# Split projections of a two-block network: the low part of each weight slice moves from VectorE to GpSimd

## The reference, cut to what matters

```python
k, v = jnp.split(mem_n @ w_kv, 2, axis=-1)                    # mkv, for both layers: 2 x (1024 x 512)
... = split_cols(h @ w_in, EVEN_SPLITS)                       # even_in: 1024 x 4096
return x + jnp.concatenate([y_a, y_b, y_m], axis=-1) @ w_out  # even_out: 1280 x 1024
return (gate * hs.astype(h.dtype)) @ w_out                    # lru_out: 1024 x 1024
return out @ w_o                                              # mla_out: 1024 x 1024

mod = (jax.nn.silu(c) @ ada_w[l] + ada_b[l])[:, None, :]      # modulation: 1024 x 6144, twice
shift, scale = jnp.split((jax.nn.silu(c) @ kv_ada_w + kv_ada_b)[:, None, :], 2, axis=-1)  # 1024 x 2048
```

## Time and profile before

| | us |
|---|---|
| median of 3 runs (range) | 2895.5 (2894.27 to 2897.55) |
| the profiled execution, its own time | 2892.08 |
| its span | 2890.4 |
| TensorE busy | 2405.4 (83%) |
| VectorE busy | 2093.0 (72%) |
| ScalarE busy | 1170.5 (40%) |
| GpSimd busy | 149.5 (5%) |

### The profile page before, as it was taken

One profiled execution on the slowest core, in us unless ns is written; L12 is line 12 of the kernel. 1 busy time (PEld: TensorE's weight loads), 2 busy tenths in 40 slices (PEclk: granted clock), 3 DMA queues, 4 the chain that ended last, 5 costly groups with the idle time before them and its releaser, 6 DMA issues. The chain is left out here.

```text
span 2890.4 us, 40401 instructions
## 1 busy us (share of the span) xinstructions
PE 2405.4 (83%) x11809; PEld 1961.6 (68%) x11809; DVE 2093.0 (72%) x4755; ACT 1170.5 (40%) x2040; POOL 149.5 (5%) x165
## 2 busy tenths in 40 slices
PE   4957892868374889999999995779479999999996
PEld 3745542737264778888888883467368888888885
DVE  4877788655669967777777774468977777777775
ACT  3526311410321854444444442351474444444443
POOL 0000000000002510000000000001430000000000
PEclk9978995789697999999999997899799999999998
DMA  6750661057230045555555553211015555555553
GB/s 236 254 207 1 222 216 72 30 189 259 76 124 1 0 153 189 189 190 190 191 192 190 193 182 106 88 59 45 0 53 194 192 192 190 189 189 189 190 191 113
DMA packets 159074, 428.05 MB, mean 148 GB/s; under 512 B 15348, under 2 KB 21776, under 8 KB 158992
## 3 DMA queue, kind: packets, MB, share of 16 engines
q1 hardware_dynamic: 158992, 427.09, 43.8%
HBM read 426.00 MB, written 1.05 MB: 148 GB/s over the span
## 5 line engine op out<-in xcount | busy, mean ns | idle before, releaser
L2133 PE MATMUL bank<-h_t_parts,u_t_high 128*128 128x512 f32 x2048 | 508.9, 391 | 10.2 <-DVE u_t_low L2219 10.2
L2133 PEld LDWEIGHTS bank<-h_t_parts,u_t_high 128*128 128x128 f32 x2048 | 386.2, 189 | 91.3 <-DVE u_t_low L2219 11.1
L2207 ACT ACTIVATE activated<-activated 128x256 f32<-128x256 f32 x256 | 107.1, 418 | 588.8 <-DVE activated L2232 588.8
L2219 DVE TENSOR_TENSOR u_t_low<-u_ring,u_t_high 128x1024 fp32r<-128x1024 f32 x256 | 312.9, 1222 | 28.2 <-ACT u_t_high L2197 16.8
L2146 PE MATMUL bank<-v_high,weighted_high 128*128 128x512 f32 x1024 | 319.4, 393 | 2.7 <-DVE weighted_low L2243 2.7
L2197 ACT ACTIVATE u_t_high<-u_ring 128x1024 fp32r<-128x1024 f32 x256 | 271.7, 1061 | 119.9 <-DMA u_ring<-in_peer_u 115.0
L2146 PE MATMUL bank<-v_low,weighted_high 128*128 128x512 f32 x1024 | 317.2, 391 | 0.0
L2146 PE MATMUL bank<-v_high,weighted_low 128*128 128x512 f32 x1024 | 316.3, 390 | 0.0
L2226 DVE TENSOR_TENSOR v_low<-v_ring,v_high 128x1024 fp32r<-128x1024 f32 x256 | 311.2, 1216 | 0.0
L2232 DVE TENSOR_REDUCE activated<-bank 128x256 f32<-128x512 f32 x256 | 177.0, 691 | 183.4 <-PE bank L2136 183.4
L2203 ACT ACTIVATE v_high<-v_ring 128x1024 fp32r<-128x1024 f32 x256 | 270.3, 1056 | 72.5 <-PE bank L2146 71.8
(11 more groups left out here) (441 smaller groups left out, 3396.2 us busy)
## 6 DMA issues: line engine op xcount, KB each, us to landing
u_ring<-in_peer_u SPq DMA_DIRECT2D x256, 512.0 KB, 4.4
v_ring<-in_peer_v SPq DMA_DIRECT2D x256, 512.0 KB, 3.6
mod_ring<-in_ada_w SPq DMA_DIRECT2D x96, 512.0 KB, 6.6
panel<-in_l_w_in SPq DMA_DIRECT2D x15, 2048.0 KB, 9.1
panel<-in_peer_w_q SPq DMA_DIRECT2D x8, 2048.0 KB, 7.7
panel<-in_l_w_out SPq DMA_DIRECT2D x4, 2560.0 KB, 9.5
panel<-in_lru_w_in SPq DMA_DIRECT2D x4, 2048.0 KB, 7.8
mod_ring<-in_kv_ada_w SPq DMA_DIRECT2D x16, 512.0 KB, 6.6
```

What stands on the lines that cost most here:

```text
L2133: nc.tensor.matmul(banks[2 + k][:, :], UTH[:, k, j, :], H2[:, j, :, :].rearrange("p a s -> p (a s)"), start=(j == 0), stop=False, skip_gro ...
L2219: nc.vector.tensor_tensor(UTL[:, s, :, :].rearrange("p a b -> p (a b)"), UR[:, s, :], UTH[:, s, :, :].rearrange("p a b -> p (a b)").bitcas ...
```

## The change: what it does

A GpSimd list is added to the block of `project_split`. For every slice it has the waits that VectorE had (the panel's load, the ring's slot, the high part), and then the same subtraction as a GpSimd instruction, which counts `w_low` up. VectorE's list keeps the source's low parts, the evacuations, the modulation steps and their sums, and no longer waits for panels, for ring slots or for high parts of weights. TensorE, ScalarE and SyncE have the same lists as before. It holds for all five stages.

```diff
@@ -528,6 +528,18 @@
                         evacuate(f, act, "a", i - 1)
                 evacuate(f, act, "a", len(ps) - 1)
 
+            @block.gpsimd
+            def _(pool):
+                for q, (i, k) in enumerate(slices):
+                    if k == 0:
+                        wait_panel(pool, ps[i])
+                    if q >= 4:
+                        wait_used(pool, q - 4)
+                    pool.wait_ge(w_high, q + 1)
+                    w = slots[ps[i] % 3][:, k * 512:(k + 1) * 512]
+                    nc.gpsimd.tensor_tensor(ring[:, q % 4, 1, :], w, ring[:, q % 4, 0, :].bitcast(F32), ALU.subtract)\
+                        .then_inc(w_low, 1)
+
             @block.vector
             def _(dve):
                 f = dve_f.on(dve)
@@ -536,14 +548,6 @@
                         dve.wait_ge(src_high, k + 1)
                         nc.vector.tensor_tensor(SL[:, k, :], src[:, k, :], SH[:, k, :].bitcast(F32), ALU.subtract)\
                             .then_inc(src_low, 1)
-                    if k == 0:
-                        wait_panel(dve, ps[i])
-                    if q >= 4:
-                        wait_used(dve, q - 4)
-                    dve.wait_ge(w_high, q + 1)
-                    w = slots[ps[i] % 3][:, k * 512:(k + 1) * 512]
-                    nc.vector.tensor_tensor(ring[:, q % 4, 1, :], w, ring[:, q % 4, 0, :].bitcast(F32), ALU.subtract)\
-                        .then_inc(w_low, 1)
                     if k == 2 and i > 0:
                         evacuate(f, dve, "v", i - 1)
                     if mod_steps:
```

## The result

| | before | after |
|---|---|---|
| median, us (range, runs) | 2896.0 (2894.3 to 2897.6, 4) | 2920.0 (2916.4 to 2923.7, 4) |
| ratio to before (95% interval) | 1 | 1.0083 (1.0066 to 1.0101) |
| span of the profiled execution, us | 2890.4 | 2914.7 |

The kernel became 24 us slower. The forecast was 37 us slower, 2932.

The account below looks back on a forecast made before the run. TensorE was taken as the bound in steady stretches, VectorE only in first panels; `even_in` +22.4, `even_out` +8.7, `lru_out` +4.3, `mkv` +0.5 and `mla_out` +1 made +37 on 2895.5, about 2932 us, range 2896 to 2965.

Parts of the forecast that it names:

- What bounds the kernel: Split projections: TensorE sets the pace in steady stretches, 1.42 us a slice; VectorE is slower only in first panels, 1.73.
- What the change removes: VectorE's queue: 132 subtractions of 0.69 us leave; worth something only in first panels and `lru_out`, nothing in `mkv`.
- The GpSimd subtraction: All five split projections: 132 added GpSimd subtractions of 128x512 at 1.22 us each, low end 1.17, high end 1.46.
- Both engines wait: Contested slices: SBUF reads of GpSimd and VectorE's two-input operations block each other, so a slice costs both engines' times added.
- The size of VectorE's share: Contested slices: after release a modulation step adds 0.65 us, L352 0.40, a source low part 0.34.
- The path in `lru_out`: `lru_out`: 16 subtractions, VectorE's steps, source parts and two adds sum to 34.7 us, ending at 821.8 against 817.5: +4.3.
- That nothing blocks: Split projections: GpSimd's 1.22 us runs beside VectorE and TensorE decides everywhere: -8, so 2887 us; chance 0.09.
- That only VectorE waits: Split projections: GpSimd never waits, steady stretches keep pace, first panels get late source parts: +3, about 2899 us; chance 0.08.
- The clock: `even_in` and `even_out`: TensorE's clock falls too, 84 slices at the lower level adding +84 more, near 3016 us; chance 0.04.

Follow-up runs that it names:

- one_input: Against the changed kernel, GpSimd copies the weight slice instead of subtracting, so the low part is not computed: 2889.3 us, ratio to before 0.9976.
- psum_acc: Against the changed kernel, the modulation's accumulator lies in PSUM for panels begun in a split projection, GpSimd keeping all low parts: 2891.6 us, ratio to before 0.9985.

## Why the prediction was right, and what was off

**What bounds the kernel: right.** TensorE is the bound in steady stretches: with the collision gone, nine slices take 12.84 us (12.80 before), and what was taken off VectorE there is worth nothing. The 24.4 us of the earlier trace rows were read too simply as all that could be taken: they add weight loads to matmuls, and leave out 18.8 us that weight loads waited for source parts from the same queue. No run came near either; one_input, the fastest, gained 6.9.

**What the change removes: undersized in one place.** `mkv` kept its wait for the modulation piece, as foreseen. In `lru_out` neither evacuation nor steps delay low parts any longer, and psum_acc and one_input show what that is worth: TensorE's stretch falls from 30.9 to 24.8 or 24.6 us, the time from VectorE's first instruction to its last from 35.3 to 30.6 or 29.3. In psum_acc that is as much as the whole gain (4.6 us), and the kernel after gives it back.

**The GpSimd subtraction: right.** 1.22 us forecast; 1.27 at its shortest, 1.31 in psum_acc. The high end of 1.46 was idle caution: the line ran through an operation of another kind.

**Both engines wait: right, and shown.** From the earlier trace rows only VectorE's side was known. GpSimd's side: 1.638 us a subtraction beside steps with two SBUF inputs, 1.308 beside steps with one. VectorE's: 1.49 against 0.754. The sum of times holds: in `even_in` GpSimd was busy 102.5 us, 64 x 1.27 = 81.3 and 21.2 of waiting. By the Trainium skill ("SBUF — State Buffer", "SBUF: two separate sides") whichever engine is second waits for the whole instruction of the first. The trace agrees on both sides: a step ends 0.56 us after the subtraction before it, a subtraction 1.14 us after the step before it. What that costs a slice is next.

**The size of VectorE's share: the term that was off.** I had 0.65 us for a step, 0.40 for L352 and 0.34 for a source part, 37.4 us in `even_in`; measured 21.2, or some 0.43 for each contested slice (1.70 less 1.27). A contested slice was to take 1.22 + 0.65 = 1.87 us; it takes 1.14 of the subtraction and 0.56 of the step. So either engine has some of its time behind it at the release: the step 0.19 of its 0.745, where I had allowed about 0.1, and the subtraction 0.13 of its 1.27, where I had allowed nothing. A source part was oversized too: in `mla_out`, where its first subtractions meet one each, two start 1.43 us apart, 0.16 more than 1.27 and not 0.34:

```profile
1942.65 1.47 POOL L540 TENSOR_TENSOR slice_parts<-panel,slice_parts 128x512 fp32r<-128x512 f32 x1
...
1944.08 1.47 POOL L540 TENSOR_TENSOR slice_parts<-panel,slice_parts 128x512 fp32r<-128x512 f32 x1
```

The overestimate of 16.2 us in `even_in` was in part made good by two other errors, the subtraction's 1.27 for 1.22 (3.2 us) and the idle time under "A term that was missing" (3.9 us); that they cancel some of it is luck. The overestimate runs through `even_in` (+22.4 forecast, +14 measured with its later first slice) and `even_out` (+8.7, +5.9), and is 11 of the 13 us between forecast and result; `lru_out` (+4.3, +2.2) has the other two.

**The path in `lru_out`: off.** The sum let the last low part wait for all of VectorE's steps. The low parts did not wait: GpSimd ran ahead, TensorE's stretch became 1.6 us shorter (29.3 for 30.9), and what grew is VectorE's own end, by 2.2 us. That it came out with the right sign is in part luck.

**A term that was missing.** In a first panel VectorE has two held operations a slice, and TensorE needs one of them. GpSimd fills its four slots and stops, TensorE waits for the source part (8.9 us of its matmuls in 13 waits over the stages, none before). GpSimd is idle meanwhile, 3.9 us in `even_in` in four gaps, and the sum did not have that. In the total the oversized share above hides it.

**The rivals.** That nothing blocks is refuted by the step of 1.77 us. That only VectorE waits is refuted by GpSimd's 1.638. The clock: `even_in` was granted 0.98 before and 0.97 after, though nine slices took 2 us longer; no fall. `lru_out` fell from 0.95 (786 to 818 us, before) to 0.90 (803 to 838, after), in a stage whose end VectorE sets; no run prices that.

```profile
82.00:192.00 110.00, 103.60 (x412) 73.53 (x412) 95.09 (x71) 53.47 (x92) 102.52 (x64) 0.97 0.78 283
```

## What to carry to other kernels

Before work goes to GpSimd, count for the stage both engines' operations that read SBUF twice (and VectorE's one-input operation from SBUF to SBUF, which was held too), and add the two sums as if they were one engine. That is the cautious figure: here 1.27 and 0.745 us made 1.70 a slice, not 2.0. If it stays under the bound, these runs give no reason to fear the move. If it doesn't, put one operand of VectorE's operation in PSUM: here that turned 24 us of loss into 4.6 us of gain (2891.6 against 2896.2) with no instruction more. And an engine that waits for another pays in its own queue too: halving GpSimd's part kept 14 of the 24 us.

## What the runs showed of the hardware that I had not expected

- A contested modulation step takes 1.67 to 1.77 us on VectorE, 0.9 to 1.0 more than alone, but costs GpSimd only some 0.43 a subtraction (1.70 against 1.27), well under the step's own 0.745.
- The modulation's first step, one input, SBUF to SBUF, is held as well: 1.50 us where it took 0.48. Written to PSUM it takes 0.74 and isn't held. Both from VectorE's timelines, after and psum_acc:

```profile
809.91 1.50 DVE L352 TENSOR_SCALAR mod_acc<-mod_ring,silu_c 128x512 f32<-128x512 f32 x1
```

```profile
83.54 0.74 DVE L358 TENSOR_SCALAR bank<-mod_ring,silu_c 128x512 f32<-128x512 f32 x1
```

- An evacuation with one input from PSUM and one from SBUF runs through beneath a GpSimd subtraction (0.69), the addition of two SBUF tensors behind it doesn't (1.35, in `mla_out` after):

```profile
1947.78 0.69 DVE L1136 TENSOR_TENSOR gated<-bank,gate_row 128x512 f32<-128x512 f32 x1 [3.38 <-PE bank L505]
1948.50 1.35 DVE L1137 TENSOR_TENSOR x_res<-gated,x_res 128x512 f32<-128x512 f32 x1
```
